# Expert loop of a two-block model: one-hot gather turned round with transposes, and a scatter of two 64-row products

## What is computed

```python
top_vals, top_idx = lax.top_k(logits, TOP_K)          # 4 of 32
gates = jax.nn.softmax(top_vals, axis=-1)
...
hcat = xblk @ w_up[e] + b_up[e]                       # 1024 -> 2048
x_glu = jnp.minimum(hcat[:, 0::2], 7.0)
x_lin = jnp.clip(hcat[:, 1::2], -7.0, 7.0)
act = x_glu * jax.nn.sigmoid(1.702 * x_glu) * (x_lin + 1.0)
y = act @ w_down[e] + b_down[e]                       # 1024 -> 1024
...
contrib = y_slots[dest] * gate_sorted[:, None]
out = jax.ops.segment_sum(contrib, tok_sorted, num_segments=N)
```

## Time and profile before

| | us |
|---|---|
| median of 3 runs | 2070.54 |
| lowest and highest | 2065.12, 2072.7 |
| the profiled execution: its time | 2066.53 |
| its span, first to last instruction | 2065.2 |
| mean granted TensorE clock | 0.975 |
| PE busy, share of the span | 94% |
| read from HBM, mean rate over the span | 535.17 MB, 260 GB/s |
| the experts' loop in the span | about 1000 to 2048 |

### The profile page before, as it was taken

One profiled execution on the slowest core, in us unless ns is written; L12 is line 12 of the kernel. 1 busy time (PEld: TensorE's weight loads), 2 busy tenths in 40 slices (PEclk: granted clock), 3 DMA queues, 4 the chain that ended last, 5 costly groups with the idle time before them and its releaser, 6 DMA issues.

```text
span 2065.2 us, 24031 instructions
## 1 busy us (share of the span) xinstructions
PE 1943.8 (94%) x9397; PEld 1119.4 (54%) x9398; DVE 729.9 (35%) x939; ACT 469.5 (23%) x522; POOL 54.5 (3%) x66
## 2 busy tenths in 40 slices
PE   7989998987999999986889999999999998999997
PEld 6768884474999775543434434434434442444443
DVE  3467762343667323633312222212212211221223
ACT  1434440241444223220111111111111110111111
POOL 0000001000000200400000000000000000000000
PEclk9999999988999999998899999999999999999999
DMA  7435452402545333313889999999999937999992
GB/s 250 149 122 195 172 204 83 156 7 82 190 178 197 128 129 122 123 41 136 352 314 402 407 408 406 413 399 413 411 405 408 410 131 314 393 409 409 406 416 112
DMA packets 125773, 537.00 MB, mean 260 GB/s; under 512 B 8688, under 2 KB 8792, under 8 KB 92920
## 3 DMA queue, kind: packets, MB, share of 16 engines
q1 hardware_dynamic: 120048, 531.64, 65.8%
q10 hardware_dynamic: 5672, 4.59, 0.8%
HBM read 535.17 MB, written 1.05 MB: 260 GB/s over the span
## 4 chain that ended last, share of the span: by engine, by line
PE 93%; DVE 4%; issue 1%; ACT 1%; ACTq 0%; DMA 0%; POOL 0%; PEldq 0%; DVEq 0%; POOLq 0%
PE psA L1530 36%; PE psB L678 9%; PE psA L689 9%; PE psB L1525 6%; PE psB L339 6%; PE psB L1555 6%; PE psB L330 5%; PE psA L352 5%; PE psA L1074 2%; PE psA L1640 1%; PE psA L1623 1%; PE psB L314 1%; PE psB L741 1%; PE psB L1081 1%; PE psA L1531 1%
## 5 line engine op out<-in xcount | busy, mean ns | idle before, releaser
L1530 PE MATMUL psA<-panel_ring,gathered_T 128*64 128x512 f32 x1024 | 446.8, 594 | 0.0
L1531 PE MATMUL psA<-panel_ring,gathered_T 128*64 128x512 f32 x1024 | 446.8, 594 | 0.0
L1530 PEld LDWEIGHTS psA<-panel_ring,gathered_T 128*64 128x64 f32 x1024 | 141.0, 138 | 294.4 <-issue 294.4
L1530 PE MATMUL psA<-panel_ring,activated_T 128*64 128x512 f32 x528 | 235.4, 599 | 0.7 <-ACT activated_T L1752 0.7
L1531 PE MATMUL psA<-panel_ring,activated_T 128*64 128x512 f32 x528 | 235.4, 599 | 0.0
L1859 DVE TENSOR_SCALAR glu<-psA 128x512 f32<-128x512 f32 x32 | 22.1, 691 | 472.8 <-PE psA L1531 472.8
L624 ACT ACTIVATE w_high<-cut 128x2048 fp32r<-128x2048 f32 x64 | 123.0, 1921 | 171.6 <-DVE cut L573 171.6
L1530 PEld LDWEIGHTS psA<-panel_ring,activated_T 128*64 128x64 f32 x528 | 70.0, 137 | 158.5 <-issue 157.6
L678 PE MATMUL psB<-hT_high,w_high 128*128 128x256 f32 x512 | 145.0, 283 | 3.7 <-DVE w_low L575 3.7
L575 DVE TENSOR_TENSOR w_low<-panel_ring,cut 128x2048 fp32r<-128x2048 f32 x64 | 146.7, 2293 | 2.2
L678 PE MATMUL psB<-hT_high,w_low 128*128 128x256 f32 x512 | 144.9, 283 | 0.0
(11 more groups left out here) (396 smaller groups left out, 2547.5 us busy)
## 6 DMA issues: line engine op xcount, KB each, us to landing
panel_ring<-in_expert_w_up SPq DMA_DIRECT2D x128, 2048.0 KB, 11.2
panel_ring<-in_expert_w_down SPq DMA_DIRECT2D x64, 2048.0 KB, 10.8
panel_ring<-in_mlp_w SPq DMA_DIRECT2D x32, 2048.0 KB, 8.1
panel_ring<-in_w_in SPq DMA_DIRECT2D x11, 2048.0 KB, 8.0
panel_ring<-in_fox_w_in SPq DMA_DIRECT2D x6, 2048.0 KB, 7.9
panel_ring<-in_lru_w_in SPq DMA_DIRECT2D x4, 2048.0 KB, 17.2
panel_ring<-in_lru_w_out SPq DMA_DIRECT2D x2, 2048.0 KB, 7.8
panel_ring<-in_fox_w_out SPq DMA_DIRECT2D x2, 2048.0 KB, 7.8
```

Source lines behind the costliest of these rows:

```text
L1530: M.matmul(ps[0:SLOTS], lhsT, rhs[0], **flags)
L1531: return M.matmul(ps[SLOTS:P], lhsT, rhs[1], **flags)
```

## The change

- `gather` is turned round: the one-hot matrix (128 tokens by 64 slots) is stationary and x moves, in two pairs of products with 512 columns each. They give token rows instead of columns: features 0 to 511 in PSUM partitions 0 to 63, features 512 to 1023 in 64 to 127. ScalarE copies them (`gathered_rows`), TensorE transposes them (`transposed`, four transposes), ScalarE copies the result (`gathered_T`, now 512 wide, before 1024).
- `scatter_tile` is two products of 64 rows each, one on rows 0 to 63, the other on rows 64 to 127 of the array, without the zeros. Both tiles now use the same two PSUM banks, so each waits for VectorE's addition of the one before.
- The gated matrix is half as large: two transposes instead of four, two VectorE instructions instead of four, a scatter matrix of 256 columns instead of 512.
- In an extra pass TensorE frees each panel when it is done with it (`frees`); the branch on the number of tokens now encloses the pass, whose code stands there twice.

```diff
-        self.iota_ab = sb("iota_ab", [P, 2, P])
-        self.ids = sb("slot_ids_ab", [P, 2, P])
-        self.one_hot = sb("one_hot", [P, TT, P])
-        self.weighted = sb("gated_one_hot", [P, 2, TT, P])
-        self.scatter = sb("scatter_matrix", [P, 2, T])
-        self.xg = sb("gathered_T", [P, KD, P])
+        self.iota_twice = sb("slot_ids_twice", [P, 2, SLOTS])
+        self.ids = sb("extra_slot_ids", [P, 2, SLOTS])
+        self.one_hot = sb("one_hot", [P, TT, SLOTS])
+        self.weighted = sb("gated_one_hot", [P, TT, P])
+        self.scatter = sb("scatter_matrix", [P, T])
+        self.xrows = sb("gathered_rows", [P, 512])
+        self.xg = sb("gathered_T", [P, 4, 2, SLOTS])
...
-        self.X, self.S = k.psB
-        self.Xg = flat(self.X[:]).rearrange("p (n s) -> p n s", s=P)
+        self.S = k.psB[0]
+        self.XR, self.XT = k.psB[1][:, 0, :], k.psB[1][:, 1, :]
...
-        for c in range(KD):
-            for tt in range(TT):
-                last = M.matmul(m.Xg[:, c, :], k.x[:, tt, c * P:(c + 1) * P], m.one_hot[:, tt, :],
-                                start=(tt == 0), stop=(tt == TT - 1))
+
+        for tt in range(TT):
+            last = halves(m.XR, m.one_hot[:, tt, :], [k.x[:, tt, c:c + 512] for c in (0, 512)],
+                          start=(tt == 0), stop=(tt == TT - 1))
+        return last
...
+    def transposed(ps, src):
+        for n in range(4):
+            last = M.transpose(ps[:, n * P:(n + 1) * P], src[:, n * P:(n + 1) * P], k.ident[:])
+        return last
+
+    def transpose_weighted(frees):
+        for tt in range(TT):
+            last = M.transpose(m.AT[:, tt * P:(tt + 1) * P], m.weighted[:, tt, :], k.ident[:])
+            if tt == 0 and frees:
+                last.then_inc(s.consumed, 1)
         return last
 
     def halves(ps, lhsT, rhs, **flags):
...
-                last = halves(m.U[:, q, :], inp[:, 2 * j + r, 0:SLOTS],
+                last = halves(m.U[:, q, :], inp[:, (2 * j + r) % 4, (2 * j + r) // 4, :],
...
-        for ab in range(2):
-            last = M.matmul(m.scatter_ps(tt)[:, ab, :], matrix[:, ab, tt * P:(tt + 1) * P], rows[:], start=True, stop=True)
+        for half in range(2):
+            r = slice(half * SLOTS, (half + 1) * SLOTS)
+            last = M.matmul(m.S[:, half, :], matrix[r, tt * P:(tt + 1) * P], rows[r, :], start=True, stop=True)
...
             up_panel(m.xg, 3).then_inc(s.up_done, 1)
             M.wait_ge(s.built, 4 + e * 2)
-            M.wait_ge(s.summed, 1 + e * 2)
+            M.wait_ge(s.rows_copied, 1 + e)
             gather().then_inc(s.gathered, 1)
             M.wait_ge(s.y_copied, 1 + e)
             M.wait_ge(s.scatter_copied, 1 + e)
+            M.wait_ge(s.summed, 1 + e * 2)
             scatter_tile(0, m.scatter, m.y).then_inc(s.scattered, 1)
             M.wait_ge(s.activated, 2 + e)
             for n in range(4):
                 last = M.transpose(m.AT[:, n * P:(n + 1) * P], m.glu[:, n * P:(n + 1) * P], k.ident[:])
-                if n == 0 and free:
+                if free and n == 0:
                     last.then_inc(s.consumed, 1)
             last.then_inc(s.act_T, 1)
-            M.wait_ge(s.gather_copied, 2 + e)
-            scatter_tile(1, m.scatter, m.y).then_inc(s.scattered, 1)
+            M.wait_ge(s.rows_copied, 2 + e)
+            transposed(m.XT, m.xrows).then_inc(s.rows_T, 1)
             M.wait_ge(s.act_copied, 2 + e)
             panel_in(4)
             last = down_panel(0)
             if free:
                 last.then_inc(s.consumed, 1)
+            M.wait_ge(s.summed, 2 + e * 2)
+            scatter_tile(1, m.scatter, m.y).then_inc(s.scattered, 1)
             panel_in(5)
             down_panel(1).then_inc(s.down_done, 1)
-            M.wait_ge(s.gated, 5 + e * 4)
-            for ab in range(2):
-                for tt in range(TT):
-                    c = (2 * ab + tt) * P
-                    last = M.transpose(m.AT[:, c:c + P], m.weighted[:, ab, tt, :], k.ident[:])
-                    if ab == tt == 0 and free:
-                        last.then_inc(s.consumed, 1)
-            last.then_inc(s.gated_T, 1)
+            M.wait_ge(s.gated, 3 + e * 2)
+            transpose_weighted(free).then_inc(s.gated_T, 1)
...
-        def one_pass(base, i):
-            dve_step = lambda n: (s.extra_dve, 15 * i + n + e * 45)
-            act_step = lambda n: (s.extra_act, 5 * i + n + e * 15)
-
-            def free(step, panels):
-                if base == SLOTS:
-                    M.wait_ge(s.extra_pe, 7 * i + step + e * 21)
-                    M.sem_inc(s.settled, 1)
-                    with M.If(tokens < 2 * SLOTS + 1):
-                        M.sem_inc(s.consumed, panels)
-
+        def one_pass(base, i, frees):
+            dve_step = lambda n: (s.extra_dve, 13 * i + n + e * 39)
+            act_step = lambda n: (s.extra_act, 6 * i + n + e * 18)
             M.wait_ge(*dve_step(3))
             gather().then_inc(s.extra_pe, 1)
+            M.wait_ge(*act_step(1))
+            transposed(m.XT, m.xrows).then_inc(s.extra_pe, 1)
             M.wait_ge(*dve_step(4))
-            M.wait_ge(*act_step(1))
+            M.wait_ge(*act_step(2))
             up_bias()
             for j in range(4):
                 last = up_panel(m.xg_x, j)
+                if frees and j < 3:
+                    last.then_inc(s.consumed, 1)
             last.then_inc(s.extra_pe, 1)
-            free(2, 4)
             M.wait_ge(*dve_step(8))
             for n in range(4):
                 last = M.transpose(m.AT[:, n * P:(n + 1) * P], m.glu[:, n * P:(n + 1) * P], k.ident[:])
+                if frees and n == 0:
+                    last.then_inc(s.consumed, 1)
             last.then_inc(s.extra_pe, 1)
-            M.wait_ge(*act_step(3))
-            down_panel(0)
+            M.wait_ge(*act_step(4))
+            last = down_panel(0)
+            if frees:
+                last.then_inc(s.consumed, 1)
             down_panel(1).then_inc(s.extra_pe, 1)
-            free(4, 2)
-            M.wait_ge(*dve_step(13))
-            M.wait_ge(*act_step(4))
-            for ab in range(2):
-                for tt in range(TT):
-                    c = (2 * ab + tt) * P
-                    last = M.transpose(m.AT[:, c:c + P], m.weighted[:, ab, tt, :], k.ident[:])
-            last.then_inc(s.extra_pe, 1)
+            M.wait_ge(*dve_step(11))
             M.wait_ge(*act_step(5))
-            for tt in range(TT):
-                scatter_tile(tt, m.scatter_x, m.y_x).then_inc(s.extra_pe, 1)
-
-        passes(M, s, e, tokens, (s.extra_pe, EXTRA["pe"]), one_pass)
+            transpose_weighted(frees).then_inc(s.extra_pe, 1)
+            M.wait_ge(*act_step(6))
+            scatter_tile(0, m.scatter_x, m.y_x).then_inc(s.extra_pe, 1)
+            M.wait_ge(*dve_step(12))
+            scatter_tile(1, m.scatter_x, m.y_x).then_inc(s.extra_pe, 1)
+
+        def pe_pass(base, i):
+            if base > SLOTS:
+                one_pass(base, i, False)
+            else:
+                with M.If(tokens < 2 * SLOTS + 1):
+                    one_pass(base, i, True)
+                with M.Else():
+                    one_pass(base, i, False)
+
+        passes(M, s, e, tokens, (s.extra_pe, EXTRA["pe"]), pe_pass)
...
-    M.wait_ge(s.gather_copied, 1 + NE)
-    M.wait_ge(s.summed, 1 + 2 * NE)
     for tt in range(TT):
+        M.wait_ge(s.summed, 1 + 2 * NE + tt)
...
         A.wait_ge(s.gathered, 2 + e)
-        A.wait_ge(s.up_done, 2 + e)
-        A.activation(m.xg[:], m.Xg[:], ACT.Copy).then_inc(s.gather_copied, 1)
+        A.activation(m.xrows[:], m.XR, ACT.Copy).then_inc(s.rows_copied, 1)
         A.wait_ge(s.act_T, 2 + e)
         A.wait_ge(s.down_done, 1 + e)
         A.activation(m.actT[:], m.at4, ACT.Copy).then_inc(s.act_copied, 1)
+        A.wait_ge(s.rows_T, 2 + e)
+        A.wait_ge(s.up_done, 2 + e)
+        A.activation(m.xg[:], m.xT, ACT.Copy).then_inc(s.gather_copied, 1)
...
             A.wait_ge(*pe_step(1))
-            A.activation(m.xg_x[:], m.Xg[:], ACT.Copy).then_inc(s.extra_act, 1)
+            A.activation(m.xrows[:], m.XR, ACT.Copy).then_inc(s.extra_act, 1)
+            A.wait_ge(*pe_step(2))
+            A.activation(m.xg_x[:], m.xT, ACT.Copy).then_inc(s.extra_act, 1)
...
-        return V.tensor_tensor(m.acc[:, tt, :], m.acc[:, tt, :], flat(m.scatter_ps(tt)[:]), ALU.add)
+        return V.tensor_tensor(m.acc[:, tt, :], m.acc[:, tt, :], flat(m.S[:]), ALU.add)
...
-        for ab in range(2):
-            for one in choose(e, m.iota_ab[:, ab, :], m.weighted[:, ab], True):
-                one.then_inc(s.gated, 1)
+        for one in choose(e, flat(m.iota_twice[:]), m.weighted, True):
+            one.then_inc(s.gated, 1)
...
-            for ab in range(2):
-                for one in choose(e, m.ids[:, ab, :], m.weighted[:, ab], True):
-                    one.then_inc(s.extra_dve, 1)
-            for tt in range(TT):
-                V.wait_ge(*pe_step(6 + tt))
```

(22 more changed lines are left out.)

53 lines of the change are left out of this document (26 added, 27 removed).

## The result

The changed kernel takes 2692.2 us (median of 4 runs, 2690.7 to 2695.4) against 2068.8 for the kernel before (also the median of 4 runs): a ratio of 1.302, 95% interval 1.300 to 1.304. The forecast was 2008. The page of the changed kernel: busy time, granted clock of the 40 slices, the queue that fetches instructions, the chain that ended last by engine, and the group of bias products that open each expert.

A forecast was written before the change was run, and what follows sets the result against it. PE was taken to set the pace at 30.85 us an expert, DMA's floor only 0.75 lower. Gains 36.2 + 0 + 25.8 + 1 = 63.0, taken as 61, brought 2066.5 to 2005.5, put at 2008 us; range 1998 to 2032.

The forecast's parts named there:

- the stall of 9.18 behind it: Behind the first expert: a wait of 9.18 us, claimed to stay because the change touches no resource behind it.
- a second such stall: At the extra pass: the new branch might cost the first expert's stall once more, making the prediction wrong by 9.
- Rival 3, the clock: Experts' loop: PE's added waits halve the clock once an expert, 31.6 against 30.85 us, about 2093 in all; chance 6%.
- PE's period: TensorE's own time for one expert in the loop: 28.2 us forecast, against 30.85 before.
- 7.02 + 0.96 + 0.3: End of each expert: down products 7.02 us, second scatter tile with switching 0.96, two gated transposes 0.3.
- switches between forms of product: TensorE in each expert: six tiling-mode switches instead of four, about 0.1 us each, two more 0.2.
- Rival 1: Scatter: 64-row products run one after the other, PE needs 29.7 us an expert, 2027 to 2030 in all; chance 13%.
- The loads: Panel loads by DMA: 30.1 us an expert, setting the pace from about the tenth expert; expert 21's last lands at 1650.4.
- Rival 2: Panel loads: 409 GB/s, or 30.85 us an expert, is the most DMA sustains; about 2027 in all; chance 12%.
- the sum behind the pass: Ten experts behind the extra pass: the loop's last load lands 328.4 us after the pass starts; gain 25.8 us.
- The extra pass: Between expert 21 and the last ten experts: 46.6 us before, change taken as 0, from -4 to +9.
- Freeing the panels singly: Extra pass: first panel freed some 11.5 us in instead of 23.7; worth nothing today, needed with DMA as the bound.

The follow-up runs named there:

- changed kernel + 64: The changed kernel with 64 idle semaphore increments on TensorE ahead of the expert loop, moving the loop 64 instructions along: 2020.0 us, 0.9754 of the kernel before.
- cured kernels: Kernels with the change but no stalls in the loop: changed kernel + 64 (2020.0 us), the one without the doubled pass (2018.5), bulk kernel + 64 (2017.7).
- bulk kernel + 64: The changed kernel without the doubled extra pass (panels freed in bulk as before), moved by 64 instructions: 2017.7 us, 0.9754 of the kernel before.
- the kernel before so moved: The kernel before, with 64 idle increments ahead of the loop and 150 in the never-taken branch for over 128 tokens: 2717.6 us.

## Why the prediction was wrong, point by point

**The step that failed** is one sentence: "the stall of 9.18 behind it has no resource behind it that the change touches, so it stays". The resource was TensorE's store of code, and the change touched it twice: the shorter gather moved the loop's start over a block edge, and the doubled pass moved the end of the skipped part into a new block. Either alone costs nothing (8 blocks each: the changed kernel + 64, and the one without the doubled pass). The profile did show it: the page's row of the instruction queue, with 40 transfers, three of which lie in that stall, and a jump (L1508) that took 7.1 us in it, where it takes 0.2 later. A wait called "issue" that happens once at the first end of a loop, together with transfers on that queue, is the first trip through code, and a change that adds a branch has to be counted against it. I had even written down a second such stall, at the extra pass and for 9 us; its place (every expert) and its size (20.2 to 22.2 but for 23.0 and 13.0 around the extra pass, and some 2 more through the clock behind it) were wrong. The profiled executions of the changed kernel and of it + 64 differ by 670.2 us: -2.5 ahead, 6.8 in the first expert, 445.2 in the next 20, 5.2 around the pass, 204.6 in the 9 behind it, 10.9 after the last activation. Of the 51.3 that an expert now takes in the median, 28.45 are its work and 22.9 the stall and its clock. No rival held it: the one on the slower side, the clock, gave 2093.

**What was right**, by the cured kernels and the unstalled parts of the changed one. PE's period 28.45, forecast 28.2. Gather, first tile and transposes in the changed kernel's timeline, [idle before <- releaser] where there is one:

```profile
1222.20 0.59 PE L1540 MATMUL psB<-x,one_hot 128*64 128x512 f32 x1
...
1224.03 1.13 PE L1566 MATMUL psB<-expert_out,scatter_matrix 64*128 64x512 f32 x4
1225.21 0.66 PE L1637 MATMUL psA<-ident,glu 128*128 128x128 f32 x4
1225.71 0.60 PE L1529 MATMUL psB<-ident,gathered_rows 128*128 128x128 f32 x4
1226.56 0.64 PE L1540 MATMUL psA<-panel_ring,activated_T 128*64 128x512 f32 x1 [0.25 <-ACT activated_T L1751]
```

Transposes start 3.0 behind the up products (2.9), down products 1.35 behind them (1.34). The down part with the second tile and the gated transposes takes 1235.22 - 1226.56 = 8.66, where I had 7.02 + 0.96 + 0.3 = 8.3: the scatter pair is 1.06, not 0.86. The other 0.2 I put down to switches between forms of product, of which I had counted six an expert; by the order of the change they are seven (before, four). No run isolates what one costs. Rival 1, products one after the other, is out.

**The loads** were right to 0.1%, and the point from which they set the pace, about the tenth expert, as well. In the changed kernel + 64 the first load for expert 2 lands at 1053.87 + 7.6 = 1061.5, and the last one for expert 21 at 1659.0: 597.5 us for 119 loads, forecast 597.1 (1053.3 to 1650.4). Rival 2 (409 GB/s as the most) is out too: 418 hold for 300 us. The 435 GB/s that the Trainium skill's page DMA: Bandwidth & Descriptors (Where 436 GB/s comes from) gives as the ceiling are not reached. (In the sum behind the pass, 62.5 + 53 x 5.02 is 328.6 and not 328.4; nothing hangs on it.)

**Where the cured kernels lie 10 to 12 over 2008.** Most of it is the same failed step on a small scale: the stall behind the first expert is 14.80 in the changed kernel + 64 (13.04 in the bulk kernel + 64) in place of 9.18. Besides, the clock's last stretch at half ahead of the loop lasted 20.48 us, in place of 13.65. Together these started the loads for expert 2 at 1061.5 in place of 1053.3, and with the loads as bound nothing gives that back. The extra pass, forecast at 0, goes either way: by the measure that gave 46.6 before it took 49.2 in the changed kernel + 64 (1664.88 to 1714.08) and 43.6 in the bulk kernel + 64 (1661.98 to 1705.62). The same stretch of it in the changed kernel + 64:

```profile
1665.00:1680.00 15.00, 11.80 (x36) 3.64 (x38) 0.81 (x4) 2.07 (x4) 0.00 (x0) 0.66 0.00 0
```

and in the bulk kernel + 64:

```profile
1662.00:1677.00 15.00, 11.79 (x58) 4.15 (x58) 0.81 (x4) 2.07 (x4) 0.00 (x0) 1.00 0.00 0
```

PE stands still at the same places and is busy 11.8 us in both, but with 36 rows of products in the one and 58 in the other: in the one the clock fell, and that pass ended 4.2 us later (38.54 against 34.32 from the activation of expert 21 to that of its pass). Why it fell in one and not in the other these runs do not tell.

**Freeing the panels singly** was to be needed once the loads set the pace. It was not: bulk or single, 2018.5 and 2020.0 with intervals that overlap. In the profiled executions bulk freeing costs at most one more expert at the loads' pace, at the very end. The doubled pass was there for this alone, so it paid nothing, and it brought one of the two blocks more, where the engine had room for one.

**Rival 3, the clock:** inside the loop of the cured kernels the clock is at its lower level only around the stall behind the first expert and around the extra pass (1.00 in both stretches of the changed kernel + 64). In the changed kernel it falls in each 21 us stall, which is a result of the fault and not its cause.

## What to carry to other kernels

Count the blocks that a loop on an engine enters, with the one behind each, whenever a change adds a branch, doubles code or shifts a loop's start: here one block more than the engine holds cost all of them, every time round. A chain with "issue" at the end of an iteration and a growing row of the instruction queue is how it looks; moving the loop by some idle instructions tells whether it is that, but by more than one distance: 64 cured it here, 24 and 256 did not. And a second resource just under the bound (here 30.12 under 30.85) sets what a good change to the first can bring: 1.7 of the 2.4 us an expert were lost to it in the second half.

## What the runs showed of the hardware

- TensorE kept 8 blocks of 256 instructions (16 KB each). 7 or 8 blocks in a loop: no transfer after the first round. 9: nine transfers an expert and in the median 18.9 us (the kernel before so moved) or 21.0 us (the changed kernel) of standing still, 2.1 to 2.3 us for each block.
- In the stall shown, four jumps to code that was not there took 4.1 to 7.3 us each; the same jumps take 0.2 in the kernel before.
- 512 positions more of never-taken code cost nothing (2016.6 us); what counts is whether its end brings in another block.
- An idle increment on TensorE costs 0.12 us: 216 of them held it 25.25, 256 held it 31.44.
- Two products of 64 rows on different rows of the array run side by side: 1.06 for the pair of 512 columns, against 1.91 for two full ones.
- A product with 64 moving columns took as long as one with 128: 3.71 against 3.77 for 16 of them, each with a 128x128 stationary. What sets it no run isolates.
- One core drew 418 GB/s for 300 us.
